# Second block of a two-block network: index projections first, its selection rounds ahead of other due steps, branch products out of rounded halves

## What is computed

```python
u = rms_norm(x, norm_g) * (1 + scale) + shift          # scale, shift, gate: c_silu @ w_ada + b_ada
z = u @ w_in                                           # 1024 -> 8772 columns
aq, ak, av, ag, iq, ik, iw, bq, bk, bv, bg, cq, ck, cv, cg, ma, mb, mc = split(z)
# a: 8 heads; each query sees its 128 best keys by an index score
score = sum_h iw[t, h] * relu(rope(iq)[t, h] . rope(ik)[s])      # causal; top 128 of 512
ya = softmax_attention(rope(aq), rope(ak), av, only the top keys) * silu(ag)
# b: 8 query heads on 2 key heads, window of 128 keys, a sink per head
yb = window_attention(rope(bq), rope(bk), bv, sinks) * silu(bg)
# c: stick-breaking attention, 8 heads
yc = stick_breaking(cq, ck, cv) * silu(cg)
merged = sigmoid(ma) * (ya @ w_br_a) + sigmoid(mb) * (yb @ w_br_b) + sigmoid(mc) * (yc @ w_br_c)
x = x + gate * (merged @ w_out)
```

## Time and profile before

| | us |
|---|---|
| median of 3 runs | 2892.8 (2892.53 to 2900.39) |
| profiled execution | 2900.88 |
| its span | 2899.0 |
| PE busy | 2750.3 (95%) |
| DVE busy | 1701.4 (59%) |
| ACT busy | 1092.2 (38%) |
| GpSimd busy | 657.2 (23%) |
| mean granted TensorE clock | 0.973 |

### The profile page before, as it was taken

The page is one execution under the profiler, slowest core; times in us unless marked ns, Lnnn a source line. Parts: engine busy times, 40 slices in busy tenths (PEclk is TensorE's granted clock), DMA queues, the critical chain, the costliest instruction groups (busy, mean ns, idle before and its releaser), DMA issues.

```text
span 2899.0 us, 36400 instructions
## 1 busy us (share of the span) xinstructions
PE 2750.3 (95%) x14752; PEld 2143.8 (74%) x14752; DVE 1701.4 (59%) x2796; ACT 1092.2 (38%) x1788; POOL 657.2 (23%) x494
## 2 busy tenths in 40 slices
PE   6899889999999998999998999979998999989997
PEld 5787668888878676788886888656666888756675
DVE  5679757876467674666555577644425247734424
ACT  2233544333233454432323563244323473244312
POOL 0000045888600004255530141000110131000110
PEclk9899989999999989999999999989999999999999
DMA  7353034454422213244433443211223223221222
GB/s 223 113 153 115 28 102 132 158 174 154 144 86 72 65 43 102 95 153 144 133 115 110 127 133 117 79 48 44 87 74 102 77 71 112 68 69 44 73 87 73
DMA packets 277381, 297.30 MB, mean 103 GB/s; under 512 B 9824, under 2 KB 259808, under 8 KB 277216
## 3 DMA queue, kind: packets, MB, share of 16 engines
q1 hardware_dynamic: 264448, 247.06, 27.3%
q0 software_dynamic: 12480, 47.45, 4.9%
q10 hardware_dynamic: 288, 0.47, 0.1%
HBM read 284.73 MB, written 2.10 MB: 99 GB/s over the span
## 4 chain that ended last, share of the span: by engine, by line
PE 89%; DVE 5%; ACT 4%; issue 1%; DMA 1%; DVEq 0%; SPq 0%; ACTq 0%
PE ps L516 87%; PE ps L699 2%; DMA raw<-in_w_in 1%; DVE hl L1272 1%; DVE s L1528 0%; DVE rawt L1272 0%; ACT recat L857 0%; ACT s L857 0%; DVE wl L1266 0%; ACT rr L857 0%; DVE recat L1489 0%; ACT att_s L857 0%; ACT att_p L857 0%; ACT wh L857 0%; DVE ca L1272 0%
## 5 line engine op out<-in xcount | busy, mean ns | idle before, releaser
L516 PE MATMUL ps<-hh,wh 128*128 128x512 f32 x2288 | 934.9, 409 | 32.1 <-DVE hl L1272 25.2
L516 PE MATMUL ps<-hh,wl 128*128 128x512 f32 x2288 | 903.2, 395 | 0.0
L516 PE MATMUL ps<-hl,wh 128*128 128x512 f32 x2288 | 902.9, 395 | 0.0
L1266 DVE TENSOR_TENSOR wl<-raw,wh 128x2048 fp32r<-128x2048 f32 (+2 forms) x186 | 463.2, 2491 | 324.6 <-ACT wh L857 324.4
L516 PEld LDWEIGHTS ps<-hh,wh 128*128 128x128 f32 x2288 | 435.4, 190 | 159.8 <-issue 55.6
L516 PEld LDWEIGHTS ps<-hh,wl 128*128 128x128 f32 x2288 | 435.3, 190 | 96.4
L516 PEld LDWEIGHTS ps<-hl,wh 128*128 128x128 f32 x2288 | 436.3, 191 | 87.5 <-issue 4.3
L857 ACT ACTIVATE wh<-raw 128x2048 fp32r<-128x2048 f32 (+2 forms) x186 | 342.5, 1841 | 222.5 <-PE ps L516 168.6
L857 ACT ACTIVATE rawt<-ps 128x512 f32<-128x512 f32 (+1 forms) x106 | 63.3, 597 | 325.0 <-PE ps L516 324.9
L1738 POOL TENSOR_TENSOR strewn<-strewn,cond 128x1024 f32<-128x1024 f32 x80 | 163.4, 2043 | 7.5 <-DMA strewn<-in_w_ada 5.9
L1272 DVE SCALAR_TENSOR_TENSOR xT<-ps,mod,xT 128x512 f32<-128x512 f32 x80 | 59.6, 749 | 165.4 <-PE ps L516 165.4
(11 more groups left out here) (232 smaller groups left out, 3935.2 us busy)
## 6 DMA issues: line engine op xcount, KB each, us to landing
raw<-in_w_in SPq DMA_DIRECT2D x74, 1024.0 KB, 5.5
raw<-in_w_up SPq DMA_DIRECT2D x44, 1024.0 KB, 5.1
strewn<-in_w_ada POOLq DMA_DIRECT2D x80, 512.0 KB, 4.1
raw<-in_w_ada SPq DMA_DIRECT2D x24, 1024.0 KB, 5.3
raw<-in_w_in SPq DMA_DIRECT2D x44, 512.0 KB, 5.2
raw<-in_w_out SPq DMA_DIRECT2D x16, 1024.0 KB, 5.3
raw<-in_w_down SPq DMA_DIRECT2D x16, 1024.0 KB, 5.3
stage<-in_w_ada SPq DMA_DIRECT2D x8, 1024.0 KB, 11.4
```

The source lines that it names most:

```text
L516: return e.matmul(o, a, b, start=start, stop=stop, skip_group_check=True)
L1266: return e.tensor_tensor(o, a, b, op)
```

## The change

Four things, in both layers of the second block:

1. The order of chunks becomes a list, `BLOCK2`, with iq and ik first; gates and pairs of c directly after bq as before; bkv after c's pairs; the copies of b's keys and values (`bkc`, `bvt`) now come after the first tile of a's gates.
2. `weave` takes its own `ahead` (0.2) and weights for this block, with 5.0 for the rounds `tr` and 0.6 for `c1` and `tm`.
3. The change of banks is a step at the end of a side list (`side_d`) instead of a main unit. c's gates and a's heads name it as their condition.
4. The branch chunks are split into `wh` and `wl` like all others, the gated y is split into a high and a low part (`gs`: a copy of ACT, a subtraction of DVE), laid over buffers that are free by then, and the products are `thrice`. Merge chunks (`am`, `bm`, `cm`) are split in two halves, and PE waits for the half it reads.

```diff
+    def mixer(self, nm, c):
+        y, low = {"a": (self.aq, self.aq_r), "b": (self.bq, self.bq_r), "c": (self.cq, self.cq_r)}[nm]
+        if nm == "c":
+            high = [self.rr_r[:, :], self.adaacc_r[:, :], self.t1s_r[:, 0, :], self.t1s_r[:, 1, :]][c]
+        else:
+            high = (self.ak_r if nm == "a" else self.av_r)[:, c, :]
+        return y[:, c, :], high, low[:, c, :]
...
-            due = [(sum(left[i]) * WEIGHT.get(sides[i][0][0][0], 1.0), when, i) for when, i in open_ if when <= self.clock["PE"] + AHEAD]
+            due = [(sum(left[i]) * weight.get(sides[i][0][0][0], 1.0), when, i) for when, i in open_ if when <= self.clock["PE"] + ahead]
...
         for kk in range(KD * x // parts_, KD * (x + 1) // parts_):
             go.wait_ge(*at("hl", tag, kk))
             for b, (key, x, c0, n) in zip(banks, tiles):
+                go.wait_ge(*at("wl", j, M.part_of(plan[j], x, kk)))
...
     def branch(l, nm, o, j, part):
-        y = {"a": M.aq, "b": M.bq, "c": M.cq}[nm]
-        b = begun(("br", l, nm, o), part[0])
-        v = M.piece(M.raw[plan[j]["slot"]], plan[j], 0)
-        go.wait_ge(*at("raw", j))
+        b, w = begun(("br", l, nm, o), part[0]), chunk(j, 0)
+        go.wait_ge(*at("wl", j))
         for kk in range(4 * part[0] // part[1], 4 * (part[0] + 1) // part[1]):
-            go.wait_ge(*at("gated", l, nm, kk))
-            m = mm(b[:, :], v[:, kk, 128 * (o % 2):128 * (o % 2) + 128], y[:, kk, :], kk == 0, kk == 3)
+            _, high, low = M.mixer(nm, kk)
+            go.wait_ge(*at("y_low", l, nm, kk))
+            m = thrice(b[:, :], w, kk, 128 * (o % 2), 128, high, low, kk == 0, kk == 3)
...
-        act(M.wh[s][:, 0:n], M.raw[p["slot"]][:, 0:n], ACT.Copy).then_inc(*up("act_wh", ("wh", j)))
+        for x, (c0, c1) in enumerate(M.split_parts(p)):
+            act(M.wh[s][:, c0:c1], M.raw[p["slot"]][:, c0:c1], ACT.Copy).then_inc(*up("act_wh", ("wh", j, x)))
...
+    def mixer_split(l, nm, c):
+        y, high, _ = M.mixer(nm, c)
+        go.wait_ge(*at("gated", l, nm, c))
...
+        act(high, y, ACT.Copy).then_inc(*up("act_y", ("y_high", l, nm, c)))
...
+    def mixer_split(l, nm, c):
+        y, high, low = M.mixer(nm, c)
+        go.wait_ge(*at("y_high", l, nm, c))
+        tt(low, y, high.bitcast(F32), ALU.subtract).then_inc(*up("dve_y", ("y_low", l, nm, c)))
...
-                         at("wl" if before["kind"] == "two" else "w_used", p["raw_before"])))
+                         at("wl", p["raw_before"])))
...
+        if nm == "bk":
+            go.wait_ge(*at("main", ("br", l, "c", KD - 1)))
...
+AHEAD2 = 0.2
+WEIGHT2 = {'s1': 2.0, 'sx': 1.5, 's2': 2.0, 'c1': 0.6, 's3': 1.5, 'tr': 5.0, 'c3': 1.0, 'tm': 0.6}
+
+BLOCK2 = [("iq", "ik", "cq0", "ck0", "cq1", "ck1", "cv0", "cv1", "aq0", "aq1", "ak0", "ak1", "av0", "av1", "bq0", "bq1",
+           "cg0", "cg1", "cm0", "cm1", "cm2", "cm3", "bkv", "ag0", "ag1", "am0", "am1", "am2", "am3",
+           "bg0", "bg1", "bm0", "bm1", "bm2", "bm3")] * 2
...
+    wide = ("banks", (0, 1, 2), (3, 7, 4, 5, 6))
...
+        elif nm == "bkv":
+            rope("bk", 0, ("bkv", l), after=[("tr", l, 3, 15, 16)])
+            main([("bv", l)], 4)
+            late += [("bkc", l), ("bvt", l)]
+        elif nm[1] == "g":
+            for c in (2 * x, 2 * x + 1):
+                main([("gate", l, nm[0], c)], 4, (nm, l, x) if c % 2 == 0 else None, [wide] if nm == "cg" else [("s3", nm[0], l, 3, 3)])
+                late.append(("gs", l, nm[0], c))
+        else:
+            tiles([("mg", l, nm[0], 2 * x + c) for c in range(2)], 4, (nm, l, x))
+            tiles([("br", l, nm[0], 2 * x + c) for c in range(2)], 2, (nm[0] + "br", l, x))
...
+    side_d.append((wide, None))
...
-        first = [("tr", l, 3, 15, 16), ("c3", l, 3, 2), ("v2", l, "av", 1, 3)] if cfg == "a" else [("bkc", l), ("bvt", l), ("s3", "a", l, 3, 3)]
+        first = [("tr", l, 3, 15, 16), wide, ("v2", l, "av", 1, 3)] if cfg == "a" else [("bkc", l), ("bvt", l), ("s3", "a", l, 3, 3)]
...
-    o.weave(mains, *sides)
+    o.weave(mains, *sides, ahead=AHEAD2, weight=WEIGHT2)
```

More of the change, by code:

```diff
@@ L352, in run, with weave @@
         return done
-    def weave(self, mains, *sides, done=()):
+    def weave(self, mains, *sides, done=(), ahead=AHEAD, weight=WEIGHT):
         done, parts = {unit: 0.0 for unit in done}, []
@@ L1817, in sync_program @@
             rope(*rest_[:3])
-        elif kind in ("split", "ada", "adap") or kind == "br" and rest_[2] % 2:
+        elif kind in ("split", "ada", "adap"):
             free.add(rest_[-1])
@@ L2046, in order_block2 @@
     o.put("banks", (0, 1), (3, 7))
-    mains = []
+    mains, late = [], []
+    wide = ("banks", (0, 1, 2), (3, 7, 4, 5, 6))
     def main(units, parts, key=None, after=None):
         mains.append((units, parts, key, after))
-    def turned(tiles, before=None):
-        for key, nm, c, c0 in tiles:
-            main([("rope", l, nm, c, c0, 128)], 4, key)
-            if before:
-                main_rest(before)
-            before = nm, c
-        return before
-    def main_rest(nc_):
-        main([("rest", l) + nc_], 1, False)
@@ L2064, in order_block2 @@
-    for nm in ("cq", "ck"):
-        for c in range(4):
-            main([("cqk", l, nm, c)], 4, (nm, l, c // 2) if c % 2 == 0 else None)
-    for x in range(2):
-        for tb in range(NT):
-            main([("v2", l, "cv", x, tb)], 2, ("cv", l, x) if tb == 0 else None)
-    before = turned([(("iq", l) if c == 0 else None, "iq", c, 128 * c) for c in range(2)])
-    main([("rope", l, "ik", 0, 0, 68)], 4, ("ik", l))
-    main_rest(before)
-    tiles = [((nm, l, c // 2) if c % 2 == 0 else None, nm, c, 128 * (c % 2)) for nm in ("aq", "ak") for c in range(4)]
@@ L2074, in order_block2 @@
-    turned(tiles[:1])
-    main([("iw", l)], 1, False)
-    main_rest(("ik", 0))
-    main([("ikc", l)], 1, False)
-    before = turned(tiles[1:], ("aq", 0))
-    for x in range(2):
-        for tb in range(NT):
-            main([("v2", l, "av", x, tb)], 2, ("av", l, x) if tb == 0 else None)
-            if x == 0 and tb == 1:
-                main_rest(before)
-    before = turned([(("bq", l, c // 2) if c % 2 == 0 else None, "bq", c, 128 * (c % 2)) for c in range(4)])
-    def gates(nm, after):
-        for x in range(2):
-            for c in (2 * x, 2 * x + 1):
-                main([("gate", l, nm, c)], 4, (nm + "g", l, x) if c % 2 == 0 else None, after if c == 0 else None)
-                if nm == "c" and c == 0:
-                    main_rest(before)
-        for x in range(4):
-            for c in range(2):
-                main([("mg", l, nm, 2 * x + c)], 4, (nm + "m", l, x) if c == 0 else None)
-            for c in range(2):
-                main([("br", l, nm, 2 * x + c)], 2, (nm + "br", l, x) if c == 0 else None)
@@ L2098, in order_block2, with tiles @@
-    main([("banks", (0, 1, 2), (3, 7, 4, 5, 6))], 1, False, [("c3", l, 3, 2)])
-    gates("c", None)
-    main([("rope", l, "bk", 0, 0, 128)], 4, ("bkv", l), [("tr", l, 3, 15, 16)])
-    main([("bv", l)], 4)
-    for unit in (("rest", l, "bk", 0), ("bkc", l), ("bvt", l)):
-        main([unit], 1, False)
-    gates("a", [("s3", "a", l, 3, 3)])
-    gates("b", [("s3", "b", l, 3, 3)])
+        while late:
+            mains.append(([late.pop(0)], 1, False, None))
+    def tiles(units, parts, key, after=None):
+        for n, unit in enumerate(units):
+            main([unit], parts, None if n else key, None if n else after)
```

85 lines of the change are left out of this document (56 added, 29 removed).

## The result

The changed kernel takes 2875.0 us (median of 5 runs, 2865.9 to 2880.5) beside 2893.2 for the kernel before in runs on the same chip: ratio 0.9922, 95% interval 0.9905 to 0.9939. It is faster by 0.8%: 18 us by the medians, 23 by the ratio. I had forecast 2828 and a range of 2806 to 2854: the direction was right, the size was not, and the value lies outside the range. The profiled execution took 2875.9 (span 2874.0).

A forecast was written before the change was run, and what follows sets the result against it. The prediction took PE, busy 95% of the span, as the bound: -34.0 for products, -46 for order, +15 of costs, -65 us in sum, giving a median of 2828, range 2806 to 2854.

The forecast's parts named there:

- The price of a product: Second block's branch products: eight plain fp32 cost 0.858 us each, three rounded 0.681, saving 0.177 on each of 192.
- on PE and so on the path: All 192 branch products of the second block: the 34.0 us saved on PE shorten the kernel by as much.
- so they are hidden: Added splits and gated copies, 23 and 28, 14 and 17 us on ACT and DVE, fall where both have room.
- The order's 46 us: Index first in the second block: a starts at 1775, its stretch without filler vanishes; ends 42 and 47, 46 taken.
- I expect the last round at 1730 to 1770: Index rounds of layer 0, second block: would end then instead of at 1856, earlier in layer 1.
- rival B: A new tail: a starts over 20 us late or b lacks filler; half of the 46 lost, 2850; chance 0.18.
- the 42 us priced: Stretches of a alone, both layers: idle 15.8 and 14.1 us, low clock 7.8 and 4.5, together 42.3.
- The start: Second block's start: ik's one tile (5.4 us) covers a whole split (5.3); cost 0 to 2 a layer, 1 taken.
- b's tail: End of b's tiles: 14 us of filler missing; cost 4 us a layer, 8 in all, bounds 0 and 28.
- C: The order changes but wins no overlap; only the cheaper products count, 2864; chance 0.07.
- part 1: Second block's branch products made of rounded parts instead of plain fp32: 34.0 us saved on PE.
- D: Slower: weight splits wait on DVE behind modulation chunks and rounds in c's phase, 2927 at 3 us a chunk; chance 0.05.

The follow-up runs named there:

- the run with the buffer held: The version with all of it, with each raw buffer's reload held back until PE has used the branch chunk in it: 2851.2 us, ratio 0.9840.
- the version with all of it: Changed kernel plus c's sum later, bkv early, modulation two chunks later, c's second high part in `nrm`, steps 1.0 us ahead: 2831.7 us, ratio 0.9782.

## Why the prediction was wrong

**The price of a product was right.** 0.177 us, 34 us in all: the pair period came out at 16.32, and the run with the buffer held puts the products at 38 us. The Trainium skill's halved rate for FP32_LOW_HIGH ("Perfetto Trace Analysis", Engine Utilization), read per product, would have made plain products the cheaper ones; the pair period and that run are against this reading. **That all 192 lie on the path was wrong.** The sentence "on PE and so on the path" failed. In before's placing only the 64 of b lie there, worth 7.5 us; the 128 of c and a are cover for a's and b's chains, and all 192 together gave 1.0001. I had seen this for b ("its filler is four pairs shorter") and charged 5.7 us of filler without drawing it through: cheaper filler saves nothing while a chain beside it sets the end. The words "so they are hidden", said of the work that the splits add, failed too in that order: with it the rounds took 10 and 14 us longer, and a began 9 and 15 us later.

**The order's 46 us were not there to be had with these settings.** The failed step is "I expect the last round at 1730 to 1770": it was 1827. I had counted DVE's idle 75 of 236 us as room for rounds. Of DVE's 64.6 us of idle time from 1583 to 1830 in after, 36.0 are one kind of wait at the head of its queue, and nothing behind can use it; in the kernel before 33.6 of the 75 were this wait, and I had not asked. That was rival B's mechanism ("c slows down behind the rounds on DVE"), turned around: the rounds stood behind c. With the sum of c queued later the last round came at 1782. Of the 42 us priced, layer 1's 18.6 came; of layer 0's 23.6 about half is still lost, 7.2 of idle and 4.1 of clock (17.06 x 0.24). A small slip beside it: a's pace by the rows is 8.0 us a tile (56.1 / 7), not 8.2; nothing hangs on it.

**The costs were too small.** The start: I took 1 us a layer and looked at ACT and DVE times alone, not at the rotation's DMA in front (the row of 8.98), the modulation chunk or the late load; it was 10.8 in layer 0. b's tail: 4 us a layer taken, bounds to 14; it is 6.2 us of idle (16.8 less 10.57, 17.0 less 10.77) and a clock of 0.57 on 10.6 busy, 4.5 more, so 10 to 11 a layer. My reason for a bound of 0, "steps move 0.2 us earlier, enough over forty steps", was false.

**A part I priced at nothing was worth 17 us in the version with all of it.** "The raw slot is freed after the split instead of after the product, which is earlier" was in the text, without the question who waits for that slot at the head of a queue. How much of it is in the 18 us of the change itself, no run shows.

**The rivals.** The result, 2875, lies beyond B (2850) and C (2864), between C and no change. B's mechanisms, a late a and a b without filler, both came; it was priced with half of one gain lost, and part 1 was left whole in it. D came once: its split behind a modulation chunk is half of the hole at the start. In c's phase it didn't come: PE has no further wait for `wl` there, and the whole splits took 2.28 us at the median, as before.

What stays open: some 6 us of layer 0, where 12 from a's stretch and 17 by price from the products stand against the hole of 10.8, the tail of 10 to 11 and a new wait of 2.3 for `ik`, and the layer still gained nothing; what slows the rounds when only the products change, DVE's added work or the planner's table; and which of the two settings, rounds first or 0.2 ahead, carries the 1.0% (only both were undone together).

## What to carry over

An edit that makes work cheaper is worth its price only where that work ends last; beside a chain of latencies it is cover, so price it again after asking what the chain then runs beside. Idle time of an engine with an ordered queue is free only for what stands ahead of the waiting instruction: before counting it, look at what the engine waits for and what is behind; the trace of the kernel before showed it here. And with a static planner look at where it places the steps before reordering anything: here one margin was worth 0.7% from 0.2 to 1.0 us, and 1.5 cost 1.5%.

## Hardware, not expected

- The first rounded matmul behind a plain fp32 product holds PE longer than its fellows. The profile of before:

```profile
1898.75 0.80 PE L516 MATMUL ps<-hh,wh 128*128 128x512 f32 x1
1899.39 0.40 PE L516 MATMUL ps<-hl,wh 128*128 128x512 f32 x1
```

0.64 us between these starts instead of 0.227, behind a branch chunk. The 6.86 us that I had put on eight plain products hold one such change: the products alone are 6.46 (2115.66 to 2122.12), 0.81 each, and the change is 0.40. So the sum was right with its parts mixed.

- Where GpSimd and DVE met on two-input instructions, either could be the one that paid. Of after, first beside a selection round, then beside a split with two inputs (1714.94 to 1717.23 on DVE):

```profile
1706.67 1.29 POOL L1756 TENSOR_TENSOR aq<-rawt,cst 128x512 f32<-128x512 f32 x1 [3.51 <-ACT rawt L883]
...
1715.62 2.76 POOL L1756 TENSOR_TENSOR ak<-rawt,cst 128x512 f32<-128x512 f32 x1 [2.96 <-ACT rawt L883]
```

The same operation took 2.76 us instead of 1.29, and the split kept its 2.29. The Trainium skill's rule on shared interfaces ("GPSIMD Engine Reference", specifications) agrees that they contend. In the kernel before it was the other way round:

```profile
1783.82 1.29 POOL L1710 TENSOR_TENSOR bq<-rawt,cst 128x512 f32<-128x512 f32 x1 [4.14 <-ACT rawt L857]
...
1783.96 1.70 DVE L1266 TENSOR_TENSOR bq<-bq,t1s 128x512 f32<-128x512 f32 x1
```

Here GpSimd kept its 1.29 and DVE took 1.70 instead of 0.69. In both pairs the one that started first kept its time; two pairs are no rule. The 1.19 us in the earlier trace rows, which rival D took for DVE's time beside GpSimd, is the mean of two such sums (1.70 and 1.67) and two undisturbed ones (0.69).
